# First panel of an encoder layer reordered on all engines, rotary tables scaled on VectorE, q turned and weights split between attention units

## The reference, cut to what matters

```python
h = rms_norm(x, norm_mix_g)
z = h @ w_in                                  # 1024 x 5632
u, v, q, k, va, gate_a, gate_b = jnp.split(z, SPLITS, axis=-1)
ya = spatial_gating_mixer(u, v, norm_v_g, w_spatial, b_spatial) @ w_proj_a
yb = window_attention(q, k, va, q_norm_g, k_norm_g, sink) @ w_proj_b
x = x + (sigmoid(gate_a) * ya + sigmoid(gate_b) * yb) @ w_out
x = x + hierarchical_moe(rms_norm(x, norm_ffn_g), ...)   # top 2 of 32 experts
```

## Time and profile before

| | |
|---|---|
| time, median of 3 runs | 2186.83 us (2183.53 to 2187.51) |
| profiled execution: its own time | 2199.12 us |
| profiled execution: span | 2197.3 us |
| TensorE matmul busy | 2094.5 us (95%) |
| VectorE, ScalarE, GpSimd busy | 1341.0, 1102.5, 524.9 us |
| chain that ended last | PE 17%, DMA 12%, DVE 2% of the span |

### The profile page before, as it was taken

The page is one execution under the profiler, slowest core; times in us unless marked ns, Lnnn a source line. Parts: engine busy times, 40 slices in busy tenths (PEclk is TensorE's granted clock), DMA queues, the critical chain, the costliest instruction groups (busy, mean ns, idle before and its releaser), DMA issues. The chain is left out here.

```text
span 2197.3 us, 30502 instructions
## 1 busy us (share of the span) xinstructions
PE 2094.5 (95%) x10292; PEld 1746.7 (79%) x10292; DVE 1341.0 (61%) x1627; ACT 1102.5 (50%) x1598; POOL 524.9 (24%) x664
## 2 busy tenths in 40 slices
PE   6999999999899999999999999669999999999997
PEld 6878888888788888897888888558877888878885
DVE  5554233465554233555543334559999999989996
ACT  3453333333452333345524223148777888878885
POOL 5142010220441011213400111011222244332342
PEclk9999999999999999999999999789999999999998
DMA  6312322443212322452122324379999989975974
GB/s 197 100 54 70 97 95 78 142 173 99 81 39 95 106 78 96 161 165 68 39 87 77 103 90 153 125 266 377 396 394 395 350 308 369 395 254 173 331 240 98
DMA packets 107789, 385.13 MB, mean 175 GB/s; under 512 B 9186, under 2 KB 15507, under 8 KB 83124
## 3 DMA queue, kind: packets, MB, share of 16 engines
q1 hardware_dynamic: 90660, 323.06, 40.0%
q0 software_dynamic: 17040, 60.88, 10.4%
HBM read 409.60 MB, written 35.13 MB: 202 GB/s over the span
## 5 line engine op out<-in xcount | busy, mean ns | idle before, releaser
L880 DVE TENSOR_TENSOR w_lo<-raw,w_hi 128x1024 fp32r<-128x1024 f32 (+1 forms) x216 | 251.3, 1189 | 302.6 <-ACT w_hi L634 302.5
L634 ACT ACTIVATE w_hi<-raw 128x1024 fp32r<-128x1024 f32 (+1 forms) x216 | 210.6, 1005 | 132.7 <-PE main L455 73.8
L453 PE MATMUL main<-e_g_hi,w_hi 128*128 128x512 f32 x576 | 237.8, 413 | 0.0
L455 PE MATMUL main<-e_g_hi,w_lo 128*128 128x512 f32 x576 | 225.9, 392 | 0.0
L454 PE MATMUL main<-e_g_lo,w_hi 128*128 128x512 f32 x576 | 225.2, 391 | 0.0
L441 PE MATMUL main<-w_hi,e_g_hi 128*128 128x512 f32 (+1 forms) x560 | 205.3, 367 | 7.2 <-DVE e_g_lo L894 7.1
L1734 DVE TENSOR_TENSOR e_d_lo<-held_wd,e_d_hi 128x2048 fp32r<-128x2048 f32 x80 | 182.5, 2290 | 32.6 <-ACT e_d_hi L1683 32.3
L443 PE MATMUL main<-w_hi,e_g_lo 128*128 128x512 f32 (+1 forms) x560 | 201.9, 360 | 0.0
L442 PE MATMUL main<-w_lo,e_g_hi 128*128 128x512 f32 (+1 forms) x560 | 201.7, 360 | 0.0
L1734 DVE TENSOR_TENSOR e_u_lo<-held_wu,e_u_hi 128x2048 fp32r<-128x2048 f32 x82 | 187.5, 2287 | 20.4 <-ACT e_u_hi L1683 20.4
L1734 DVE TENSOR_TENSOR e_g_lo<-held_wg,e_g_hi 128x2048 fp32r<-128x2048 f32 x80 | 182.9, 2287 | 19.3 <-ACT e_g_hi L1683 19.2
(11 more groups left out here) (297 smaller groups left out, 4773.2 us busy)
## 6 DMA issues: line engine op xcount, KB each, us to landing
held_wg<-w_gate_e SPq DMA_DIRECT2D x84, 1024.0 KB
held_wu<-w_up_e SPq DMA_DIRECT2D x84, 1024.0 KB
held_wd<-w_down_e SPq DMA_DIRECT2D x82, 1024.0 KB
raw<-w_in SPq DMA_DIRECT2D x120, 512.0 KB, 3.6
raw<-w_proj_b SPq DMA_DIRECT2D x24, 512.0 KB, 3.6
raw<-w_proj_a SPq DMA_DIRECT2D x24, 512.0 KB, 3.6
raw<-w_out SPq DMA_DIRECT2D x24, 512.0 KB, 3.7
raw<-w_in SPq DMA_DIRECT2D x24, 256.0 KB, 4.4
```

Source lines behind the costliest of these rows:

```text
L453: pe.matmul(bank[:], hi[:, k, :], mov_hi[:, k, :], start=(k == 0), stop=False)
L455: mm = pe.matmul(bank[:], lo[:, k, :], mov_hi[:, k, :], start=False, stop=(k == KT - 1))
L634: act.activation(hi, buf, ACT.Copy).then_inc(w_hi_done, 1)
L880: dve.tensor_tensor(lo, buf, hi.bitcast(F32), ALU.subtract).then_inc(w_split, 1)
```

## The change

Four things are moved, and a few instructions with them.

1. The first panel. The first x tile is scaled in two halves, straight from the accumulator banks that hold the gain row; ScalarE then copies the gain row for the later tiles. Weight quarters and halves of the first transposed tile alternate on ScalarE and VectorE. Transposes of x tiles 1 to 3 are done within the K tiles and no more ahead of them. SyncE loads weight quarters 2 and 3 ahead of x tiles 1 to 3.
2. The rotary tables of group 0 are multiplied by the gains on VectorE, a tile at a time, and no more on GpSimd.
3. GpSimd makes the four `rsk` (key norms) of group 0 ahead of its eleven late loads and the zero fill, and no more behind them.
4. In the gate-B panels one weight quarter stands before the first attention unit and one behind the second, where two stood before the first (tiles 1 and 2: one behind the second unit). q turns 4 to 7 go between `k` steps (`Q_STEPS`), into the gate product's other bank.

```diff
+        Q_STEPS = {0: {2: 4}, 1: {2: 5, 5: 6}, 2: {2: 7}}
         def q_bank(i):
-            return pt_bank[i % 2] if i >= GT else aux[2 + i % 2]
+            if i < GT:
+                return aux[2 + i % 2]
+            tile = next(j for j, steps in Q_STEPS.items() if i in steps.values())
+            return main[(tile + 1) % 2]
+        def gate_steps(p, j):
+            units = list(slots_of(4 * (p - PGB) + j))
+            steps = [("unit", s) for s in units]
+            quarters = [("split", q) for q in SPLIT_AT[p][j]]
+            if len(quarters) == 2:
+                steps.insert(2, quarters[1])
+                steps.insert(0, quarters[0])
+            elif quarters:
+                steps.insert(2, quarters[0])
+            for k, i in (Q_STEPS.get(j, {}) if p == PGB else {}).items():
+                steps.insert(steps.index(("unit", units[k * len(units) // KT])), ("q", i))
+            return steps
...
                 load_quarter(1)
-                load_x(1)
                 load_quarter(2)
                 load_quarter(3)
+                load_x(1)
...
+                            def turn_q(k, p=p, j=j):
+                                if p == PGB and k in Q_STEPS.get(j, {}):
+                                    qT_tile(g, Q_STEPS[j][k])
+                            def ready(k, p=p, j=j, first=first):
+                                if g == 0 and p == PK and j < 3 and k == (0 if j else 4):
+                                    transpose_h(0, j + 1)
...
                                 if j == 0:
                                     transpose_h(0, 0)
-                                    transpose_h(0, 1)
-                                elif j < 3:
-                                    transpose_h(0, j + 1)
...
-                            if p == PGB:
-                                qT_tile(g, 4 + j)
...
+                split_hi(2)
+                h_hi(0, 0, (0,))
+                split_hi(3)
+                h_hi(0, 0, (1,))
                 square_x(0, 1)
-                split_hi(2)
-                split_hi(3)
+                act.wait_ge(xn_ready, 1)
+                for b in range(2):
+                    act.activation(g_row[:, b * 512:(b + 1) * 512], main[b][:], ACT.Copy).then_inc(g_row_done, 1)
...
+                dve.wait_ge(rsx_ready, 1)
                 for b in range(2):
+                    c = slice(b * 512, (b + 1) * 512)
                     dve.wait_ge(g_row_ps, b + 1)
-                    dve.tensor_copy(g_row[:, b * 512:(b + 1) * 512], main[b][:]).then_inc(g_row_done, 1)
-                norm_x(0, 0)
-                split_lo(0)
-                split_lo(1)
+                    dve.scalar_tensor_tensor(out=xn[:, 0, c], in0=xn[:, 0, c], scalar=rsx[:, 0:1], in1=main[b][:],
+                                             op0=ALU.mult, op1=ALU.mult).then_inc(xn_ready if b else xn_half, 1)
+                    split_lo(b)
+                h_lo(0, 0, (0,))
+                split_lo(2)
+                h_lo(0, 0, (1,))
+                split_lo(3)
                 norm_x(0, 1)
...
+                def gain_k_tile(t):
+                    if t == 0:
+                        dve.wait_ge(rope_k_in, 64)
+                    dve.tensor_tensor(rope_k[:, t, :, :], rope_k[:, t, :, :], gain_k, ALU.mult).then_inc(rope_set, 1)
+                    dve.wait_ge(rope_set, t + 1)
...
                 norm_x(0, 1)
-                gain_tables(0, 5, "k")
                 norm_x(0, 2)
+                norm_x(0, 3)
                 tables(0, 4, "q")
-                norm_x(0, 3)
                 pool.dma_start(ws, a["w_spatial"].rearrange("g p q -> p g q")).then_inc(ws_in, 16)
+                for t in KV_TILES[0]:
+                    norm_k(0, t)
```

More of the change, by code:

```diff
@@ L815, in _ @@
                                 copy_qT(g, j)
-                            if p == PGB:
-                                copy_qT(g, 4 + j)
                             if p in (PGB, PGB + 1):
-                                for s in slots_of(4 * (p - PGB) + j):
-                                    attend(g, s)
+                                for what, n in gate_steps(p, j):
+                                    if what == "unit":
+                                        attend(g, n)
+                                    elif what == "split":
+                                        split_hi((g * NP + p + 1) * NQ + n)
+                                    else:
+                                        copy_qT(g, n)
                             if g and p == PPB and j == 1:
@@ L888, in norm_x, with h_lo @@
                                              op0=ALU.mult, op1=ALU.mult).then_inc(xn_ready, 1)
-                def h_lo(g, t):
-                    for b in range(2):
+                def h_lo(g, t, halves=range(2)):
+                    for b in halves:
                         dve.wait_ge(hT_hi_done, 2 * GT * g + 2 * t + b + 1)
@@ L1186, in _ @@
                             if p in (PGB, PGB + 1):
-                                for s in slots_of(4 * (p - PGB) + j):
-                                    attend(g, s)
+                                for what, n in gate_steps(p, j):
+                                    if what == "unit":
+                                        attend(g, n)
+                                    elif what == "split":
+                                        split_lo((g * NP + p + 1) * NQ + n)
                             if g and p == PPB and j == 1:
@@ L1267, in norm_x, with norm_k @@
                     rms(rsx[:, t:t + 1], ssx[:, t:t + 1], 1, D).then_inc(rsx_ready, 1)
+                def norm_k(g, t):
+                    pool.wait_ge(head_squared, head_at(g, None, t))
+                    rms(rsk[:, t, :], ssk[:, t, :], 2, HD).then_inc(rsk_ready, 1)
                 def norm_f(g, t):
@@ L1331, in _ @@
                         norm_f(g - 1, 3)
-                    for t in KV_TILES[g]:
-                        pool.wait_ge(head_squared, head_at(g, None, t))
-                        rms(rsk[:, t, :], ssk[:, t, :], 2, HD).then_inc(rsk_ready, 1)
-                    if g == 0:
-                        gain_tables(0, 4, "q")
+                    if g:
+                        for t in KV_TILES[g]:
+                            norm_k(g, t)
                     for q in range(2):
```

74 lines of the change are left out of this document (48 added, 26 removed).

## The result

The changed kernel takes 2174.49 us, the median of 7 runs (2167.14 to 2177.3); the kernel before, run beside it, 2193.09 (2183.53 to 2196.05). The ratio is 0.9924, with a 95% interval from 0.9904 to 0.9944: 12 to 21 us less. The forecast's 2168 was made against 2186.8; its 18.5 off the 2193.1 measured beside it would be 2174.6. The profiled execution took 2175.61, 1.1 above that median, and its span is 2173.5.

A forecast was written before the change was run, and what follows sets the result against it. TensorE, busy 95% of the span, was taken as the bound, so only its idle or half-clock time could go. Start 12.5 plus gates 6 off 2199.1 gave 2180.6; the profiled execution's 12.3 off too, 2168.3 us, range 2162 to 2176.

The forecast's parts named there:

- the last of the sum: Whole kernel: the profiled execution is 12.3 above the unprofiled median, so the same difference comes off 2186.8, giving 2168.3.
- the start: First panel up to the first VA product: 12.5 us gained, with bounds of 9 and 14.2.
- the gate part: Gate panels of the three groups: 1.9 + 1.9 + 2.2 = 6 us gained, with bounds of 0 and 12.
- First product at 13.0: First panel: TensorE's first K product comes at 13.0 and not 18.09, after waiting for `main[0]`; 5.1 us gained.
- The order of loads charged as a cost of up to 0.7: First panel, SyncE: two weight quarters pass x tile 1, which may cost at most 0.7 of the start.
- Wait of 1.4 at tile 2, none at tile 3, VA at 31.5: First panel: TensorE waits 1.4 for `h_lo` at tile 2, none at tile 3, which ends at 31.5; before, VA began at 44.02.
- Slack of 4 for Q's last quarter: Q's last weight quarter lands at 42 to 43, is split at 44 and wanted at 48; nothing charged.
- the collision rival: Late loads and weight quarters collide, TensorE waits for Q's or VA's last quarter; some 6 back, 2175 to 2178; chance 0.06.
- Gate tile 0: Gate panels' first tile: scores 2 wait falls to 0.3 to 0.5, new 1.8 wait at scores 4; 0.1 to 0.3 gained in group 0.
- The rival that the quarters eat the gate part: Gate panels: quarters between units cost what the q turns give; gate part 0, 2174; chance 0.14.
- Clock falls at tile 2: First panel, rival: half clock behind tile 2's pause costs 2 us, the start gives 10.5; 2170; chance 0.2.
- The weighed rule: First panel: the clock falls only after a pause longer than 2.07 or 1.4, so tile 2's pause costs nothing more.

The follow-up runs named there:

- start only: The changed kernel with its gate part undone: both quarters and the q turn ahead of the units, q turn in the old banks; 2176.83 us, ratio 0.994.
- typical runs: Five variants of the changed kernel with its gate code untouched, whose group 1 takes 462.3 to 463.0 us and group 2 445.8 to 446.1.
- quarters ahead: The changed kernel with all gate-panel weight quarters ahead of the tile's first unit, q turns left where they are; 2167.21 us, ratio 0.9899.
- gate-only run: The kernel before with only the change's gate part (quarters between units, q turns moved to the other bank); 2182.49 us, ratio 0.9963.
- three together: The changed kernel with quarters ahead of the first unit, group 1's table loads behind GpSimd's units and `h_lo` one tile earlier; 2166.61 us, ratio 0.9891.
- norms only: The kernel before with only group 0's four key norms moved ahead of the late loads on GpSimd; 2185.65 us, ratio 0.9968.
- tables behind units: The changed kernel with group 1's eight table loads moved behind GpSimd's 32 attention units; 2165.78 us, ratio 0.9893.

## Why the prediction came out as it did

**The step that failed is the last of the sum**, by which the profiled execution's 12.3 above the median comes off again ("so the same difference comes off 2186.8: 2168.3"). In the changed kernel the profiled execution took 2175.61 and the median of 7 runs is 2174.49: 1.1, not 12.3. In the kernel before it was 2199.12 against 2193.09: 6.0. The median 2186.8 came from 3 runs, and the 7 beside the change are 6.3 above it. So 2168.3 was 6.2 too low, and 2174.5 lies in the range near its upper end. The 12.3 was no constant of the kernel. The rest of the program, which no run edits, scatters over 1072 to 1085 us and is wide enough to make it; that this is where it came from no run shows.

Against its own base the sum was too small. The forecast for the profiled execution was 2180.6, and it took 2175.6. By the marks the start gave 13.6 (forecast 12.5), the gate part 6.9 (2.8, 2.4, 1.7; forecast 6), and the rest 3.3, which the change doesn't touch. The medians differ by 18.6, nearly the 18.5 of the forecast. That is luck: in the profiled executions the same difference is 23.5. Faster, the sign, was right.

Point by point:

- **First product at 13.0**: 12.76. Its chain is right, the wait for `main[0]` at its end too, and the halves are shown by an experiment (1.4 net). "Waits for `h_lo` together under 2" was not met by the rows' labels (3.8), since that wait for the bank is put down to `h_lo`. **The order of loads charged as a cost of up to 0.7**: wrong sign. It gives 1.3 at the first product, since ScalarE waits for the third quarter and x tile 1 has time.
- **Wait of 1.4 at tile 2, none at tile 3, VA at 31.5**: 1.41, none, 30.66.
- **Table products hidden on VectorE**: shown. What the prediction didn't price is that leaving them on GpSimd costs 3.9, the half clock behind the longer pause among it.
- **Slack of 4 for Q's last quarter**: 0.9. ScalarE got it at 44.14 (forecast 42 to 43), VectorE ended at 46.46 (44), and TensorE wanted it at 47.36 (48). The rows:

```profile
44.14 1.06 ACT L661 ACTIVATE w_hi<-raw 128x1024 fp32r<-128x1024 f32 x1 [4.97 <-DMA raw<-w_in]
...
45.23 1.23 DVE L919 TENSOR_TENSOR w_lo<-raw,w_hi 128x1024 fp32r<-128x1024 f32 x1 [5.57 <-ACT w_hi L661]
...
47.36 0.39 PE L465 MATMUL main<-w_hi,e_g_hi 128*128 128x512 f32 x1
```

  This was the least safe term: the collision rival, given 0.06, was 0.9 us away in this execution.
- **Gate tile 0**: scores 2 at 0.3 to 0.5 and a new wait of 1.8 were 0.27 and 1.41; group 1's wait of 3 to 4 was 4.47, with half clock. Mechanism right, sizes near.
- **Gate part 6 in all**: mis-sized inside, by two errors that nearly cancel. The prediction had 8.4 for the waits of the q turns and let tile 0's quarters take 2.4 of it. The q turns give 10.4, most of the excess in group 1; there the half clock is gone too, but that the q turns ended it isn't shown, since in start only the clock fell at about 558.6, ahead of the first q turn that waits (562.41). The quarters take 2.2 against typical runs, as counted, and 5.3 against the profiled one: the difference is the clock, long in group 1 and fallen in group 2. The rival that the quarters eat the gate part named the right mechanism; it took part of the gain and not all.
- **Clock falls at tile 2**: it didn't. It fell where the forecast hadn't looked, in group 2, and cost 1.6 there. "The clock was lost behind each pause" misreads: it was lost once, at 30.95, and was still at half when the pause of 5.02 began. The weighed rule of the Trainium skill, page "TensorE: Matmul & The Clock Gate", section "HAM oscillation — how this bites in real kernels", wants a pause longer than 2.07. At tile 2 the trace agrees with it; the falls behind 2.07 and behind 1.56 and 1.19 don't.

## What to carry to other kernels

Cut a trace at marks that end each stage and compare stage by stage over several variants: here that resolved 0.3 us in group 0 where medians scatter by 5, and it showed how far a part that nobody edited scatters. Read the granted clock beside each mark before taking a difference: equal code with equal pauses differed by 1.5 to 1.8 by the clock alone. Don't carry the gap between one profiled execution and a median over to a changed kernel: it was 12.3, 6.0 and 1.1 here. On an engine that issues DMAs, put a small operation that another engine waits for ahead of the issues, and give the late loads a place where only loads stand behind them. Removing a wait that stands among other pauses can be worth little while the clock falls all the same; try the edits together before dropping one.

## What the runs showed of the hardware

- **The clock behind short pauses isn't settled by their length.** Eight executions have in group 2 the pauses of 1.5 and 1.2 with about 2.4 between their ends. Two fell to lower windows (the changed and the gate-only run) and lost 1.6; six stayed at 1.00. In group 1 pauses of 1.41 and 2.74 (quarters ahead) and 1.40 and 1.13 (three together) brought no fall; 1.35 and 2.75 in the same places (before, norms only, start only) did, and so did 1.12 and 1.40 (tables behind units), to the 1.2 GHz level. Nor is the length of the stretch settled: with the same pauses of 0.27 and 4.45 it was long in two executions and about half that in five. What decides between them stays open; no run was made to vary it alone.
- **VectorE beside GpSimd.** The scaling of 1.28 took 3.90 when it began 0.06 behind a GpSimd product of 2.87, and GpSimd's next operation of 0.19 took 1.05 beside the scaling's end. The Trainium skill's page "Trainium Architecture — The Big Picture", section "What this means for kernel authors", calls what the two share an exclusive lock and not a split of bandwidth; the trace agrees, since 3.90 is nearly the whole product and the scaling's own time one after the other. In the kernel before, the scaling began first, at 15.13, and kept its 1.28; the product that began at 15.37 took 3.82.
- **GpSimd pays for a DMA issue by time on its own queue**: 0.60 for one, 1.59 for three in the rows of group 1, 4.4 for all eight. Moved behind the units, they took the pause from 4.47 to 1.12.
